# A four-layer transformer block in one kernel: the second mixer reordered, its attention beside a projection, and down projections with 512 moving columns

## The reference, cut to what matters

```python
for layer in range(2):
    h = rms_norm(x, mix_pre_g[layer])
    m = mixer_ab(h, ...) if layer % 2 == 0 else mixer_cd(h, positions, ...)
    x = x + rms_norm(m, mix_post_g[layer])
    h = rms_norm(x, ffn_pre_g[layer])
    f = channel_mixer(h, ...)     # up 2048->8192, 3-tap conv, gelu(gate)*val, down 4096->2048
    x = x + rms_norm(f, ffn_post_g[layer])

def mixer_cd(h, positions, ...):
    c_q, c_kv, k_rope, x_lru, y_gate = split(h @ w_in, [512, 256, 64, 1024, 1024])
    c_out = mla_attention(c_q, c_kv, k_rope, ...)   # 8 heads of 128+64, chunked causal mask
    d_out = rg_lru_branch(x_lru, y_gate, ...)       # 4-tap conv, two gates, linear recurrence, gelu gate
    return concatenate([c_out, d_out]) @ w_out      # 2048 -> 2048
```

## Time and profile before

| | |
|---|---|
| median of 3 runs | 3106.29 us (3105.44 to 3106.66) |
| the profiled execution | 3105.97 us |
| its span | 3104.1 us |
| granted TensorE clock, mean | 0.964 |
| PE / PEld / DVE / ACT / POOL busy | 2897.4 / 2766.9 / 1851.9 / 1359.1 / 292.7 us |
| matmuls | 22538 |
| second mixer, first to last matmul of its projections | 1051.3 to 1442.6 us |
| down projection, layer 0 and layer 1 | 839.3 to 1026.5 us, 1847.0 to 2033.9 us |

### The profile page before, as it was taken

The page is one execution under the profiler, slowest core; times in us unless marked ns, Lnnn a source line. Parts: engine busy times, 40 slices in busy tenths (PEclk is TensorE's granted clock), DMA queues, the critical chain, the costliest instruction groups (busy, mean ns, idle before and its releaser), DMA issues.

```text
span 3104.1 us, 58351 instructions
## 1 busy us (share of the span) xinstructions
PE 2897.4 (93%) x22538; PEld 2766.9 (89%) x22538; DVE 1851.9 (60%) x2663; ACT 1359.1 (44%) x1947; POOL 292.7 (9%) x318
## 2 busy tenths in 40 slices
PE   6999989999999896788999999989999999999998
PEld 6998879999999796577999999979979998997998
DVE  4466567666544667536766654467567656666654
ACT  4444544444344454334444334444445535434643
POOL 0040012222200000000222220000000000000000
PEclk9999999999999998679999999989999999999999
DMA  5544435555555353223555555535444454544443
GB/s 187 180 141 162 143 115 169 181 184 179 166 184 180 112 170 102 68 95 122 169 183 182 182 165 183 182 114 164 162 152 156 145 183 135 167 159 143 156 162 124
DMA packets 131193, 481.73 MB, mean 155 GB/s; under 512 B 14560, under 2 KB 14688, under 8 KB 130784
## 3 DMA queue, kind: packets, MB, share of 16 engines
q1 hardware_dynamic: 130464, 475.06, 46.1%
q10 hardware_dynamic: 576, 4.47, 0.4%
HBM read 477.38 MB, written 2.10 MB: 154 GB/s over the span
## 4 chain that ended last, share of the span: by engine, by line
PE 84%; DVE 9%; ACT 3%; issue 2%; DMA 1%; POOL 0%; ACTq 0%; SPq 0%; DVEq 0%; POOLq 0%
PE BANK L455 71%; PE BANK L471 6%; ACT WHI L823 1%; DVE TM L1234 1%; DVE WLO L1159 1%; PE BANK L571 1%; DVE HLO L1237 1%; DVE X L1249 1%; DVE TM L1248 1%; PE BANK L771 1%; DVE TM L1221 1%; PE BANK L608 1%; PE BANK L638 1%; PE BANK L462 1%; DMA RING<-w 1%
## 5 line engine op out<-in xcount | busy, mean ns | idle before, releaser
L1159 DVE TENSOR_TENSOR WLO<-RING,WHI 128x1024 fp32r<-128x1024 f32 x902 | 1115.2, 1237 | 972.3 <-ACT WHI L823 971.0
L455 PE MATMUL BANK<-HHI,WHI 128*128 128x256 f32 x4768 | 1380.6, 290 | 41.9 <-DVE HLO L1237 26.5
L823 ACT ACTIVATE WHI<-RING 128x1024 fp32r<-128x1024 f32 x902 | 953.0, 1057 | 1027.5 <-PE BANK L455 877.3
L455 PE MATMUL BANK<-HLO,WHI 128*128 128x256 f32 x4768 | 1357.6, 285 | 0.0
L455 PE MATMUL BANK<-HHI,WLO 128*128 128x256 f32 x4768 | 1356.8, 285 | 0.0
L455 PEld LDWEIGHTS BANK<-HHI,WHI 128*128 128x128 f32 x4768 | 922.1, 193 | 63.2 <-issue 39.7
L455 PEld LDWEIGHTS BANK<-HLO,WHI 128*128 128x128 f32 x4768 | 924.3, 194 | 1.9 <-issue 1.0
L455 PEld LDWEIGHTS BANK<-HHI,WLO 128*128 128x128 f32 x4768 | 923.6, 194 | 0.0
L455 PE MATMUL BANK<-BIGR,WHI 128*128 128x256 f32 x3520 | 646.7, 286 | 27.2 <-POOL BIGR L1745 10.5
L455 PEld LDWEIGHTS BANK<-BIGR,WHI 128*128 128x128 f32 x3520 | 556.6, 194 | 31.2 <-POOL BIGR L1745 10.9
L455 PE MATMUL BANK<-BIGR,WLO 128*128 128x256 f32 x1760 | 502.1, 285 | 0.0
(11 more groups left out here) (277 smaller groups left out, 1822.1 us busy)
## 6 DMA issues: line engine op xcount, KB each, us to landing
RING<-w SPq DMA_DIRECT2D x902, 512.0 KB, 3.3
X<-xT ACTq DMA_DIRECT2D x1, 2048.0 KB, 9.6
outT<-M SPq DMA_DIRECT2D x4, 512.0 KB, 2.6
TB<-tab ACTq DMA_DIRECT2D x1, 1536.5 KB, 16.5
V<-vec ACTq DMA_DIRECT2D x1, 652.0 KB, 12.0
POS<-pos ACTq DMA_DIRECT2D x1, 128.0 KB, 17.6
```

The costliest lines, as they stand in the source:

```text
L455: last = mm(bank[:, 0:T], wt[s][:, kk, :], x, start=start and n == 0, stop=stop and n == 2)
L823: A(WHI[at % SPLIT][:, :, :], RING[at % RAW][:, :].rearrange("p (k n) -> p k n", k=UB), ACT.Copy)\
L1159: TT(WLO[at % SPLIT][:, :, :], RING[at % RAW][:, :].rearrange("p (k n) -> p k n", k=UB), WHI[at % SPLIT][:, :, :].bitcast(f32), ALU.subtra ...
```

## The change

1. **Order of the second mixer.** RUN_C comes first, then RUN_X, the short runs of the up projections, the gates (`lru`), RUN_Y. The norms, conv, RoPE, recurrence, gated output and attention become side generators from `mixer_cd` on, at given ticks. The three `meet`s go, and the `drain` at the end of a unit in `short` too.
2. **Attention.** `attend` and class `Attention` go; the 8 MLA heads use the `heads` pipeline of the other attentions, from tick 58 on, which is in RUN_LRU.
3. **Output projection** in three passes of K: RUN_LRU (the 8 blocks of the recurrence's half, ACT copies the sums to M), then FIRST_HEADS (heads 0 to 3) and LAST_HEADS (heads 4 to 7), whose sums DVE adds to M.
4. **Recurrence.** With a = exp(log_a) the argument is -(a*a + 1) * tanh(log_a); the reciprocal over 8 tiles goes. The gates, sums and scan are done in halves or pairs of tiles.
5. **Down projections.** High and low halves of a hidden tile are moved in one matmul of 512 columns against WHI, and WLO takes 256 columns into the second half of the bank; DVE adds the two halves of the bank into M, and ACT squares from M. PE waits for each hidden tile when it first needs it.
6. **First mixer.** The indexer begins with an empty step on each engine (after the padding of the keys on DVE), and its attention at tick 10 instead of 8; the low half of a head is made one step earlier.

The amount of projection work is the same: 90 units in the second mixer.

```diff
             e.mixer_cd()
+            e.run(RUN_C)
             e.run(RUN_X)
-            e.run(RUN_C, e.conv)
+            e.queries()
             e.lru()
-            e.run(RUN_Y, e.states)
-            e.meet()
-            e.mla_norm()
-            e.lru_out()
-            e.mla()
-            e.meet()
-            e.attend("mla")
-            e.meet()
-            e.run(RUN_MIX)
+            e.run(RUN_Y)
+            e.run(RUN_LRU)
+            e.first_heads()
+            e.attended()
+            e.last_heads()
...
+            def product_wide(bank, s, kk, x2, start, stop):
+                mm(bank[:, :], WHI[s][:, kk, :], x2, start=start, stop=False)
+                return mm(bank[:, T:2 * T], WLO[s][:, kk, :], x2[:, 0, :], start=False, stop=stop)
...
                 if r.src == "HID":
-                    pe.wait_ge(sem("hid_lo"), step_no(c, "hid", FF_T))
+                    hid = step_no(c, "hid", FF_T) - FF_T
...
+                            if r.src == "HID" and isinstance(i, int) and i == 0 and j == 0:
+                                pe.wait_ge(sem("hid_lo"), hid + k + 1)
...
-                        pe.drain().then_inc(sem("unit_used"), 1)
+                        last.then_inc(sem("unit_used"), 1)
+                        tick(c)
+                    else:
+                        last.then_inc(sem("short_out"), 2 if r.form == "v" else 1)
...
             def index(l, o0):
+                yield
                 pe.wait_ge(sem("bank_free"), o0)
...
+            def mixer_cd():
+                o0 = c["output"]
+                k0 = o0 + RUN_C.n + RUN_X.n + Q_RUN.n + KN_RUN.n
+                c["side"] = together(later(10, mla_norm()), later(31, rope_mla(o0)),
+                                     later(58, heads("mla", 0, k0, k0 + KV_RUN.n)))
...
-            def attend_beside(kind):
+            def attend():
                 o0 = c["output"]
-                c["side"] = later(8, heads("dsa", 0, o0, o0 + 4))
+                c["side"] = later(10, heads("dsa", 0, o0, o0 + 4))
...
                     if r.src == "HEADS":
                         m = M[:, i * BANKS + j, :]
                         TT(m, m, bank[:, 0:T], ALU.add).then_inc(sem("bank_free"), 1)
+                    if r.src == "HID":
+                        v.tensor_reduce(M[:, i * BANKS + j, :], bank[:, :].rearrange("p (a t) -> p t a", a=2), AX.X, ALU.add)\
+                            .then_inc(sem("bank_free"), 1)
...
+            def states():
+                part = lambda at, half: BIG[:, at + half:at + half + 4, :]
+                for half, to in zip((0, 4), CD_SQ):
+                    dve.wait_ge(sem("lru_a"), half + 4)
+                    then(TT(BIG[:, to:to + 4, :], part(CD_A, half), part(CD_A, half), ALU.mult))
+                    yield
+                for half, sq in zip((0, 4), CD_SQ):
+                    dve.wait_ge(sem("lru_a"), 8 + half + 4)
+                    STT(part(CD_GR, half), BIG[:, sq:sq + 4, :], 1.0, M[:, 8 + half:12 + half, :], ALU.add, ALU.mult)\
+                        .then_inc(sem("lru_m2"), 1)
+                    yield
...
+            def mixer_cd():
+                o0 = c["output"]
+                c["side"] = together(constants(), later(12, mla_norm()), later(21, conv(o0 + RUN_C.n)),
+                                     later(31, rope_mla()), later(44, states()), later(55, lru_out()),
+                                     later(58, heads("mla", 0)))
+
+            def add_partial(m, bank):
+                TT(M[:, m, :], M[:, m, :], bank[:, 0:T], ALU.add).then_inc(sem("bank_free"), 1)
```

More of the change, by code:

```diff
@@ L341, in later, with rest @@
             yield from part
+        def rest(n):
+            for _ in range(n):
+                yield
         def together(*parts):
@@ L770, in heads @@
                             for j in range(a.sets):
-                                last = mm(a.bank(t, j), *a.operands(k, t, j), start=True, stop=True)
+                                parts = a.operands(k, t, j)
+                                for i, (q, key) in enumerate(parts):
+                                    last = mm(a.bank(t, j), q, key, start=i == 0, stop=i == len(parts) - 1)
                         last.then_inc(sem("p_scored"), 1)
@@ new lines, in lru_out @@
+            def lru_out(o0):
+                for n, N, gap in ((0, 4, 4), (4, 7, 2), (7, 8, 0)):
+                    act.wait_ge(sem("bank_free"), o0 + N)
+                    y = BIG[:, CD_YG + n:CD_YG + N, :]
+                    A(y, y, ACT.Gelu_apprx_tanh).then_inc(sem("lru_gelu"), 1)
+                    if n == 7:
+                        hi(4, 7, 2)
+                        hi(7, 8, 3)
+                    yield from rest(gap)
+                    if n == 0:
+                        hi(0, 4, 1)
@@ new lines, in hi @@
+            def hi(n, N, done):
+                act.wait_ge(sem("lru_out"), done)
+                A(BIGR[:, CD_A + n:CD_A + N, :], BIG[:, CD_GR + n:CD_GR + N, :], ACT.Copy).then_inc(sem("lru_hi"), 1)
+            def mixer_cd():
+                o0 = c["output"]
+                y0 = o0 + RUN_C.n + RUN_X.n + Q_RUN.n + KN_RUN.n + KV_RUN.n + LRU_RUN.n
+                free = c["unit"] + sum(r.units for r in (RUN_C, RUN_X, RUN_Y)) + 12
+                c["side"] = together(later(1, constants()), later(9, mla_norm(o0)), later(23, conv()), later(42, states()),
+                                     later(51, lru_out(y0)), later(58, heads("mla", 0, free)))
@@ L1029, in log_gates, with last_heads, leave @@
+            def last_heads():
+                g0, o0 = c["m_outputs"], c["output"]
+                c["m_outputs"] = g0 + 16
+                def leave(m, bank):
+                    act.wait_ge(sem("sq_added"), g0 + m - 3)
+                    act.wait_ge(sem("bank_free"), o0 + m + 1)
+                    A(TM[:, m % 4, :], M[:, m, :], ACT.Square).then_inc(sem("sq_done"), 1)
+                short(LAST_HEADS, leave)
             def log_gates(l):
@@ L1076, in heads @@
                 c["heads"] = h0 + a.n
-                for k in range(a.n + (3 if kind == "dsa" else 1)):
+                for k in range(a.n + (3 if a.split else 1)):
+                    if a.split and k >= 3:
+                        act.wait_ge(sem("p_head_taken"), h0 + k - 2)
+                        if k == 3:
+                            act.wait_ge(sem("unit_used"), free)
+                        A(HHI[:, k - 3, :], a.out(k - 3), ACT.Copy).then_inc(sem("p_head_hi"), 1)
                     for _ in range(a.units // 2):
@@ L1093, in heads, with attend @@
                         A(turned_flat(h), BANK[6][:, 0:3 * P], ACT.Copy).then_inc(sem("p_turned_out"), 1)
-                    if kind == "dsa" and k >= 3:
-                        act.wait_ge(sem("p_head_taken"), h0 + k - 2)
-                        if k == 3:
-                            act.wait_ge(sem("unit_used"), free)
-                        A(HHI[:, k - 3, :], a.out(k - 3), ACT.Copy).then_inc(sem("p_head_hi"), 1)
                     for _ in range(a.units // 2):
                         yield
-            def attend_beside(kind):
-                c["side"] = later(8, heads("dsa", 0, c["unit"] + RUN_V.units))
-            def attended():
-                drain_side(c)
+            def attend():
+                c["side"] = later(10, heads("dsa", 0, c["unit"] + RUN_V.units))
             def gate(group, l, g0):
@@ L1391, in states, with lru_out @@
+            def lru_out():
+                gated(0, 4, 1)
                 yield
-                r, i, th = (BIG[:, at:at + 8, :] for at in (CD_GR, CD_GI, CD_XLO))
-                then(TT(i, i, M[:, 0:8, :], ALU.mult))
+                gated(4, 7, 2)
+                low_half(0, 4, 1)
                 yield
-                dve.wait_ge(sem("lru_a"), 2)
-                den = M[:, 8:16, :]
-                then(TS(den, th, -1.0, 1.0, ALU.mult, ALU.add))
-                yield
-                then(v.reciprocal(den, den))
```

628 lines of the change are left out of this document (288 added, 340 removed).

## The result

The changed kernel takes 2997.07 us (median of 4 runs, 2996.87 to 2997.58); before, it was 3106.47 us (4 runs, 3105.44 to 3106.86). The ratio is 0.965, with a 95% interval from 0.9636 to 0.9665. The forecast was 2986 us, with a range from 2965 to 3012: right in direction and within the range, 11 us too low. The profiled execution has a span of 2995.0 us, against 3104.1: 109.1 us less.

The account below looks back on a forecast made before the run. PE's matmuls plus PE's waits were taken to bound the kernel. Savings of 27.9 (down projections), 6.1 (indexer) and 86.0 us (second mixer) sum to 120.0: 3105.97 - 120.0 gives 2986 us, range 2965 to 3012.

Parts of the forecast that it names:

- Indexer: First mixer's indexer: the empty step removes PE's padded-keys wait and half clock, 7.5 us; last top-8 round costs 1.4; net 6.1.
- Start of the down projections: Down projections: waiting per hidden tile hides PE's 5.24 us idle behind three units, and the clock need not fall.
- The wide matmul: Down projections: a 512-column matmul takes 227 ns, so a block falls from 358.5 to 346.5 ns, 12.3 us over two layers.
- Tail of the down projections: End of each down run: DVE's addition before ACT's square takes 0.9 us, bounds 0.5 and 1.5; 1.8 us lost in all.
- Second mixer: The 90 units keep 258.2 us; with added terms 304.8 against 391.3 us, 86.5 saved.
- small matmuls: Second mixer: eleven fp32 matmuls of 256 columns (six sums, five RoPE) cost 0.44 us each, 4.8 us.
- RUN_LRU's start: Second mixer: PE waits for a chain from RUN_Y's last gate tile, 3 us, bounds 0 and 7.
- the eight heads: Second mixer's MLA attention beside projections: 3.1 us per head, 24.8 for eight; bounds 2.44 and 4 per head.
- Norm behind the mixer: End of second mixer: DVE's addition stands ahead of ACT's square, 0.5 us lost; other additions lie beside 24 of 32 units.
- the waits move in: Rival: late side work in each engine's stream also holds WHI or WLO; mixer 325 us, total 3006 us; chance 0.17.
- Columns alone: Rival, down projections: columns alone set matmul time, so the wide form gives nothing; 2998 us; chance 0.10.
- WLO becomes the bound: Rival: DVE's side-list waits delay `low`; once PE's 8 us lead is gone, units pay in full; 3121 us; chance 0.03.

Follow-up runs that it names:

- The run with the weights first: Changed kernel, but in last_heads ACT rounds the next unit's weights before squaring that unit's two outputs, instead of after; 2992.10 us.
- the last run: Changed kernel plus down-projection matmuls by unit, weights rounded before squares in last_heads and layer 0's RUN_HEADS, two top-8 rounds in one step; 2986.12 us.

## Why the forecast was right, and where it was off

- **Indexer.** 7.4 us against 6.1. Both terms were about right. PE's same product starts 0.1 us apart in the traces of before and after at 155 us and 7.9 at 250, so the stop and the half clock behind it cost 7.8 us (7.5 forecast); at the start of the short run (259.06 us) the distance is 6.4, so the last top-8 round takes 1.45 back (1.4 forecast). The missing 0.9 is won between there and the norm behind layer 0's mixer (452.5 us). The clock falls at other moments in the two traces there, and the attention begins two ticks later; I haven't separated these.
- **Start of the down projections.** As forecast: the first wide matmul starts 0.12 us behind the up run's last, and the clock stays at 1.00.
- **The wide matmul.** This is the step that failed in size: "a block goes from 3 x 119.5 = 358.5 to 227 + 119.5 = 346.5 ns". Both prices were right by themselves (226.7 and 120.0 measured), but they were read where matmuls of one width follow each other. Alternating costs 6.6 ns per block, half of the 13.3 that the form would otherwise bring; over both layers it is 6.8 us. The Trainium skill (TensorE: Matmul & The Clock Gate, Back-to-back issue gap) gives N/2.4 + 2.5 ns for the warm gap of an isolated matmul, 109 and 216 ns; the runs have 120.0 and 226.7 in a stream, so its fixed part is too small here. Its sum of 2.6 us for the wide form and the row's 12.3 lie on either side of the 6.8 measured.
- **Tail of the down projections.** DVE's addition takes 0.69 us, where 0.9 was assumed; 0.6 us of the tail were lost in layer 0. Right.
- **Second mixer.** 304.95 us against 304.8. By terms: the 2160 matmuls at 120.0 are 259.2 (258.2 forecast). The rest is counted as what the distance of two products has above 120.0 ns: 5.4 us at the first output (6 forecast); 9.6 from there to the end of the gates at 1171 us, where small matmuls (4.8), gates (5) and the norms of c_q and c_kv (3) were put at 12.8; 6.5 at RUN_LRU's start, a wait of 4.3 us and then half clock (3, bounds 0 and 7); 23.0 for the eight heads (24.8); and 1.3 for the two waits in the last pass, which the forecast didn't have. The total is better than its terms: 5.8 us more and 5.6 us less than forecast nearly cancel, and that was luck.
- **Norm behind the mixer.** "0.5 lost" was 4.8. The forecast looked at the chain behind the last output, and called the 32 additions hidden beside 24 of 32 units. It didn't ask how DVE's addition, ACT's square, ACT's rounding and DVE's low half stand in their two streams in the last pass. They form a ring of 3.69 us per unit against PE's 2.88. No busy share shows it: in the last 28.3 us of the mixer DVE is busy for 17.5 and ACT for 12.4, and yet both are late. The run with the weights first gave 3.7 us back; in the traces it is 2.5 of the norm's 4.8, and 1.3 in the mixer. The norm's other 2.3 us are not the ring. With the weights first PE's statistics still come 4.2 us behind its last product, and 1.6 before (1442.44 to 1444.07): two outputs end together now, and pass two additions, two squares behind a rounding, and two sums of POOL.
- **The rest.** 1.0 us in the hybrid layers, not looked into.

Wide form (6.6 us with its tails), norm (4.3), the rest (1.0) and mixer (0.3), less the indexer's 1.3, are the 10.9 us between 120.0 forecast and 109.1. Of the rivals, "the waits move in" would have shown at WLO in the mixer, and PE has no wait for WLO there; but it happened in small in the last pass, on the engines behind PE and in two short waits of PE. "Columns alone" would have left 360 ns per block; the time is within 1 us of this rival's 2998, but by chance: the wide form gave 6.8 us, and some 4 of the missing 11 lie in the norm. "WLO becomes the bound" did not occur; the run with the reciprocal shows how near it was: two operations of 6.55 us in neighbouring ticks cost 11.6 us.

## What to carry to other kernels

Where two engines hand work to each other twice in a loop, add up the ring (here 3.69 us), not the busy shares: the engine that feeds the bound one should issue what the loop needs next ahead of what only the end needs. Work that waits on a chain belongs beside a projection: the same eight heads cost 3.1 us each there and 7.6 us alone. Take the price of an instruction from rows with the neighbours that it will have.

## What the runs showed of the hardware

At granted clock 1.00 each matmul costs its columns and a fixed part: 120.0 ns for 256 columns and 226.7 for 512. At the upper level of 2.4 GHz these are 288 and 544 cycles, the columns and 32 more. At granted clock 0.50 the fixed part can't be seen: 256 columns take 213 ns (the run with the reciprocal, starts from 1206.07 to 1210.12 us) and 512 take 427 (the q run of the last run, 266.93 to 272.05 us), which at 1.2 GHz are the columns alone. So half clock cost 93 ns per matmul of 256 columns, and not another 120.

I had not expected that two neighbours of different width cost extra: a wide and a narrow one in alternation take 353.3 ns, 848 cycles, 16 more than the sum of the two. Sorting removes some 60% of it: 349.2 ns with two changes per sixteen matmuls, where the sum is 346.7. Why, the runs don't show; the place of the moving operand isn't the cause. Two pieces of 256 columns that lie 32 tiles apart stream as fast as one piece of 512.
